# The start of a two-block decoder: memory loaded by whole rows, the identity made on GpSimd, fewer unread products

## The reference, cut to what matters

```python
def rms_norm(x, g):
    xf = x.astype(jnp.float32)
    y = xf * lax.rsqrt(jnp.mean(xf * xf, axis=-1, keepdims=True) + EPS)
    return (y * g.astype(jnp.float32)).astype(x.dtype)
...
def memory_cross_attention(h, m, w_q, w_kv, q_qk_g, k_qk_g, w_o):
    ...
    kv = m @ w_kv
    k = rms_norm(kv[..., :D_MODEL].reshape(B, M, CROSS_HEADS, CROSS_HEAD_DIM), k_qk_g)
    v = kv[..., D_MODEL:].reshape(B, M, CROSS_HEADS, CROSS_HEAD_DIM)
    ...
def first_block(x, mem, positions, ...):
    h = rms_norm(x, attn_norm_g[l])
    proj = h @ w_in[l]
    ...
    x = x + jnp.concatenate([a_out, r_out], axis=-1) @ w_out[l]
    hc = rms_norm(x, cross_norm_g[l])
    m = rms_norm(mem, mem_norm_g[l])
    x = x + memory_cross_attention(hc, m, ...)
    hm = rms_norm(x, moe_norm_g[l])
    x = x + hierarchical_moe(hm, ...)
    return x
```

## Time and profile before

| | us |
|---|---|
| median of 3 runs (939.34 to 940.17) | 940.09 |
| the execution in the profile | 939.83 |
| its span | 937.9 |
| TensorE busy in the span | 928.7 |
| VectorE busy | 743.3 |
| ScalarE busy | 625.3 |
| GpSimd busy | 20.6 |

### The profile page before, as it was taken

One profiled execution on the slowest core, in us unless ns is written; L12 is line 12 of the kernel. 1 busy time (PEld: TensorE's weight loads), 2 busy tenths in 40 slices (PEclk: granted clock), 3 DMA queues, 4 the chain that ended last, 5 costly groups with the idle time before them and its releaser, 6 DMA issues.

```text
span 937.9 us, 13604 instructions
## 1 busy us (share of the span) xinstructions
PE 928.7 (99%) x5027; PEld 804.2 (86%) x5027; DVE 743.3 (79%) x1111; ACT 625.3 (67%) x953; POOL 20.6 (2%) x41
## 2 busy tenths in 40 slices
PE   9999999999999999999999999999999999999997
PEld 7888888888888888888888899999998888888886
DVE  6668686678899999999999889898887655555576
ACT  6785686676878788788778765847574544434456
POOL 2500000000000000000000000000000000000000
PEclk9999999999999999999999999999999999999999
DMA  9865427513799999999998364837457566555531
GB/s 337 245 184 186 146 90 246 186 62 135 247 356 392 352 363 378 354 358 376 341 383 310 103 206 143 258 114 234 154 184 245 178 195 201 185 182 179 184 130 45
DMA packets 102766, 214.50 MB, mean 229 GB/s; under 512 B 5672, under 2 KB 60480, under 8 KB 97088
## 3 DMA queue, kind: packets, MB, share of 16 engines
q1 hardware_dynamic: 101072, 211.70, 64.9%
q0 software_dynamic: 1344, 2.01, 0.8%
q10 hardware_dynamic: 304, 0.20, 0.1%
HBM read 212.84 MB, written 1.05 MB: 228 GB/s over the span
## 4 chain that ended last, share of the span: by engine, by line
PE 92%; DVE 3%; DMA 2%; ACT 1%; SPq 0%; issue 0%; DVEq 0%; ACTq 0%
PE bank L2362 20%; PE bank L2360 20%; PE bank L2361 20%; PE bank L3184 6%; PE bank L3183 6%; PE bank L3182 6%; PE bank L2377 4%; DMA stage<-in_cross_w_kv_dram 2%; PE bank L2373 2%; PE bank L2367 2%; PE bank L2368 1%; PE bank L2714 1%; PE bank L3208 0%; PE bank L3209 0%; PE bank L3210 0%; DVE w_lo L467 0%
## 5 line engine op out<-in xcount | busy, mean ns | idle before, releaser
L2360 PE MATMUL bank<-w_hi,xT_hi 128*128 128x512 f32 (+2 forms) x594 | 234.5, 395 | 0.0
L2362 PE MATMUL bank<-w_hi,xT_lo 128*128 128x512 f32 (+2 forms) x594 | 230.0, 387 | 0.0
L2361 PE MATMUL bank<-w_lo,xT_hi 128*128 128x512 f32 (+2 forms) x594 | 229.7, 387 | 0.0
L465 DVE TENSOR_TENSOR w_lo<-stage,w_hi 128x1024 fp32r<-128x1024 f32 (+3 forms) x94 | 107.5, 1143 | 30.4 <-ACT w_hi L451 29.0
L2362 PEld LDWEIGHTS bank<-w_hi,xT_lo 128*128 128x128 f32 x594 | 111.6, 188 | 22.8
L2360 PEld LDWEIGHTS bank<-w_hi,xT_hi 128*128 128x128 f32 x594 | 112.1, 189 | 20.7 <-DVE w_lo L467 0.2
L2361 PEld LDWEIGHTS bank<-w_lo,xT_hi 128*128 128x128 f32 x594 | 111.8, 188 | 20.8
L3182 PE MATMUL bank<-xT_hi,w_hi 128*128 128x256 f32 x440 | 124.6, 283 | 0.0
L3183 PE MATMUL bank<-xT_lo,w_hi 128*128 128x256 f32 x440 | 124.5, 283 | 0.0
L3184 PE MATMUL bank<-xT_hi,w_lo 128*128 128x256 f32 x440 | 124.5, 283 | 0.0
L451 ACT ACTIVATE w_hi<-stage 128x1024 fp32r<-128x1024 f32 (+3 forms) x96 | 95.5, 995 | 31.4 <-PE bank L2362 13.3
(11 more groups left out here) (492 smaller groups left out, 1579.4 us busy)
## 6 DMA issues: line engine op xcount, KB each, us to landing
stage<-in_w_in_dram SPq DMA_DIRECT2D x36, 1024.0 KB, 5.2
stage<-in_w_gate_up_dram SPq DMA_DIRECT2D x44, 512.0 KB, 4.7
stage<-in_expert_w_gate_dram SPq DMA_DIRECT2D x33, 512.0 KB, 5.4
stage<-in_expert_w_up_dram SPq DMA_DIRECT2D x33, 512.0 KB, 6.5
second<-in_expert_w_down_dram SPq DMA_DIRECT2D x16, 1024.0 KB, 6.5
stage<-in_expert_w_down_dram SPq DMA_DIRECT2D x15, 1024.0 KB, 6.9
stage<-in_w_down_dram SPq DMA_DIRECT2D x11, 1024.0 KB, 4.8
stage<-in_w_out_dram SPq DMA_DIRECT2D x8, 1024.0 KB, 5.1
```

The source lines that it names most:

```text
L465: nc.vector.tensor_tensor(w_lo[:, s, 0:half], src[:, 0:half], w_hi[:, s, 0:half].bitcast(F32), ALU.subtract)
L2360: mm(o, k_hi, v_hi, start=start, stop=False)
L2361: mm(o, k_hi, v_lo, start=False, stop=False)
L2362: return mm(o, k_lo, v_hi, start=False, stop=stop)
```

## The change

- The identity is no longer loaded. GpSimd makes it in place: AFFINE_SELECT takes ones from `one_col` where row equals column and 0 elsewhere, behind a wait for `one_col`.
- The memory comes in two whole row tiles (4 KB per row) in the place of two column halves, both at the head of SyncE's queue. `mem_loaded0` and `mem_loaded1` are now the two row tiles.
- The first quarter of the first weights goes from SyncE's queue to ScalarE's, behind the gain.
- TensorE's first unread products are 6 in the place of 8. It waits for the identity (`ones_set` 2) and for the gain, turns the gain, then turns column blocks 0 to 3 of row tile 0 and, after its landing, of row tile 1. The 2 unread products behind these turns are gone, and the turns of blocks 4 to 7 wait for no load.
- The other waits on `ones_set` count one more.

```diff
--- before.py
+++ after.py
@@ -570,8 +570,6 @@
     def row(v):
         return v.rearrange("(o n) -> o n", o=1)
 
-    first_loads = [(ident, a["const"][:, 0:P]),
-                   (mem_gain_in, a["mem_norm_g"][0].rearrange("(k p) -> k p", p=P))]
     small_loads = [(const[:, P:], a["const"][:, P:])]
     for n, g in enumerate(("attn_norm_g", "cross_norm_g", "moe_norm_g", "g_mix_2", "g_ffn_2", "g_ple_2")):
         small_loads.append((gain_in[KD * n:KD * n + KD], a[g][0].rearrange("(k p) -> k p", p=P)))
@@ -866,22 +864,22 @@
     def store(eng, t, at):
         eng.dma_start(out[0].rearrange("(t p) d -> p t d", p=P)[:, t, at], embed[:, t, at]).then_inc(sem("stored"), 16)
 
+    def first_blocks(eng, k, n):
+        return eng.dma_start(stage[:, 0, 512 * k:512 * (k + n)].rearrange("p (k n) -> p k n", k=n), before[0][0][:, k:k + n])
+
     block = ctx.enter_context(nc.Block())
 
 
     @block.sync
     def _(sp):
-        def memory(c):
-            at = slice(512 * c, 512 * c + 512)
-            sp.dma_start(xs[:, :, at], a["mem"][0].rearrange("(t p) d -> p t d", p=P)[:, :, at]).then_inc(sem(f"mem_loaded{c}"), 16)
+        def memory(t):
+            sp.dma_start(xs[:, t], a["mem"][0][P * t:P * t + P]).then_inc(sem(f"mem_loaded{t}"), 16)
 
         def first_unit(k, n, landed):
-            sp.dma_start(stage[:, 0, 512 * k:512 * (k + n)].rearrange("p (k n) -> p k n", k=n), before[0][0][:, k:k + n])\
-                .then_inc(landed, 16)
-
-        memory(0)
-        first_unit(0, 1, main.landed[0])
-        memory(1)
+            first_blocks(sp, k, n).then_inc(landed, 16)
+
+        for t in range(T):
+            memory(t)
         first_unit(1, 1, main.up_landed[1])
         first_unit(2, 2, main.up_landed[0])
         load_unit(sp, *before[1], 1)
@@ -956,6 +954,9 @@
     @block.gpsimd
     def _(pool):
         nc.gpsimd.memset(one_col[:], 1.0).then_inc(sem("ones_set"), 1)
+        pool.wait_ge(sem("ones_set"), 1)
+        nc.gpsimd.affine_select(out=ident, in_=one_col[:].to_broadcast([P, P]), pattern=[[-1, P]], compare_op=ALU.is_equal,
+                                fill=0.0, base=0, channel_multiplier=1).then_inc(sem("ones_set"), 1)
         pool.wait_ge(sem("x_loaded"), 16)
         for dst, src in small_loads:
             pool.dma_start(dst, src).then_inc(sem("constants_loaded"), 16)
@@ -977,8 +978,8 @@
 
     @block.scalar
     def _(act):
-        for dst, src in first_loads:
-            act.dma_start(dst, src).then_inc(sem("first_loaded"), 16)
+        act.dma_start(mem_gain_in, a["mem_norm_g"][0].rearrange("(k p) -> k p", p=P)).then_inc(sem("mem_gain_loaded"), 16)
+        first_blocks(act, 0, 1).then_inc(main.landed[0], 16)
 
         chain = [0]
 
@@ -1385,7 +1386,7 @@
                 for k in range(KD):
                     act.wait_ge(sem("expert_xg_lo"), bank_parts(k))
                     nc.scalar.activation(later[:, k, 0:T * P], part(k), ACT.Copy, scale=gather_g[:, k:k + 1]).then_inc(sem("later_kept"), 1)
-                act.wait_ge(sem("ones_set"), 3)
+                act.wait_ge(sem("ones_set"), 4)
             first_of = {}
 
             def gates_of(n, at):
@@ -2433,7 +2434,7 @@
             for k in range(4):
                 kk, n, at = 4 * u + k, 2 * u + k // 2, quarter(u, k)
                 if (u, k) == (0, 1):
-                    turn("mem", xs, [("mem_loaded1", 16)], (2, 3))
+                    turn("mem", xs, [], (2, 3))
                 quarter_hi_ready(pe, u, k)
                 high_ready(pe, "mem", n)
                 for t, o in enumerate(outs):
@@ -2522,12 +2523,22 @@
             fills(nc.tensor.transpose(b[:, 0:rows], gain_in, ident[0:rows, 0:rows]), "gains")
 
         pe.wait_ge(sem("unread_set"), 1)
-        unread(8)
-        pe.wait_ge(sem("first_loaded"), 16 * len(first_loads))
+        unread(6)
+        pe.wait_ge(sem("ones_set"), 2)
+        pe.wait_ge(sem("mem_gain_loaded"), 16)
         b = to_fill(pe, "mem_gain")
         fills(nc.tensor.transpose(b[:, 0:KD], mem_gain_in, ident[0:KD, 0:KD]), "mem_gain")
-        turn("mem", xs, [("mem_loaded0", 16)], (0, 1))
-        unread(2)
+        for n in range(2):
+            to_fill(pe, f"mem{n}")
+        view = xs[:].rearrange("p t (k q) -> p t k q", k=KD)
+        for t in range(T):
+            pe.wait_ge(sem(f"mem_loaded{t}"), 16)
+            for n in range(2):
+                b = bank[where[f"mem{n}"][0]]
+                for j in range(2):
+                    ins = transpose(b[:, 256 * j + P * t:256 * j + P * t + P], view[:, t, 2 * n + j])
+                if t == T - 1:
+                    fills(ins, f"mem{n}")
         for c in range(4):
             if c == 0:
                 for u in range(2):
@@ -2625,7 +2636,7 @@
             mm(o, qT_n[:, h, q], kT_n[:, h, keys], start=True, stop=False)
             return mm(o, qT_r[:, h, q], kT_r[:, h // 2, keys], start=False, stop=True)
 
-        pe.wait_ge(sem("ones_set"), 2)
+        pe.wait_ge(sem("ones_set"), 3)
         b = to_fill(pe, "s0")
         for h in range(HEADS):
             ins = score(b[:, P * h:P * h + P], h, slice(0, P), slice(0, P))
```

## The result

| | before | after |
|---|---|---|
| median of 22 runs each, us | 939.84 | 941.60 |
| lowest to highest, us | 939.34 to 941.24 | 940.44 to 943.28 |
| profiled execution: time, span, us | 939.83, 937.9 | 942.47, 940.4 |

The ratio is 1.002, with a 95% interval of 1.0014 to 1.0026: the change costs 1.8 us, where I had forecast 5. It lies inside the range (940.8 to 949.0). The interval lies wholly above 1, so it is slower, but by so little that it still lies inside what I had called the same (938.2 to 942.0).

What follows compares the result with a forecast made beforehand. TensorE, busy 99%, bounds the kernel, so the start of its real products and their clock count. 3.7 + 0.4 + 0 + 1.2 - 0.2 = +5.1 us on 939.8 gave 944.9, stated as 945.0, range 940.8 to 949.0.

Steps and rivals of the forecast that it cites:

- Identity on GpSimd: At the start: a code load before AFFINE_SELECT makes the identity ready at about 9.2, TensorE restarting 3.7 us later.
- the sign against this term: For the identity: AFFINE_SELECT starting within 2 us of the start; for the clock: first real products following at 0.23.
- Memory by whole rows: Start loads: second tile lands between 6.9 and 7.96, before the identity at 9.2, so costs nothing by itself.
- Order of the turns: Memory's first transposes: bank 5 fills after the sixth, not the fourth, so first eviction and product come 0.4 us later.
- Unread products: TensorE's start: taking away two behind the turns gains nothing, and two fewer ahead change nothing.
- Clock: First real products, 12.0 to 14.5: low clock after TensorE's standstill, 0.43 for 0.23 per product, costing 1.2 us.
- a stand of 4.6 us: TensorE idle from 4.54, after its six unread products, until the identity is ready at about 9.2.
- Given back: TensorE's wait for ScalarE at 49.07: a later TensorE finds ScalarE done, winning back 0.2 us.
- the main term: The start's wait for GpSimd's identity, priced with an 8.0 us code load: TensorE restarts 3.7 us later.
- Rival A: Start: code load nothing or short, memory's second tile sets the start; +1.4 start, 1.6 clock, less 0.2: 942.6; chance 0.24.
- Rival B: As the memory-last case, but memory lands by 6.9 to 7.5 and clock is high: 940.4 to 941.0; chance 0.16.
- Slower 0.77: Chance of a measurably slower whole kernel: 0.43 forecast case, 0.14 dearer code load, 0.20 from the memory-last case.

Runs made afterwards that it cites:

- x3_ident: Kernel before with only the identity made by GpSimd's select instead of loaded: 939.65 us, ratio 0.9998.
- x11_rows: Kernel before with memory by whole rows and the weights' first quarter on SyncE's queue behind both tiles, all else as before: 940.53 us, ratio 1.0009.
- x10_fill2: Changed kernel with the 2 unread products put back behind the memory's first turns (6 ahead, 2 behind): 940.23 us, ratio 1.0006.
- x13_ahead8: Changed kernel with 8 unread products ahead of the memory's first turns instead of 6, none behind: 940.26 us, ratio 1.0008.
- x1_fill4: Changed kernel with 4 unread products added behind the memory's first turns: 940.54 us, ratio 1.0008.
- x2_q0sp: Changed kernel with the weights' first quarter back on SyncE's queue, right behind the two memory tiles: 941.54 us, ratio 1.0018.
- x4_q0sp_fill4: Changed kernel with the weights' first quarter on SyncE's queue behind the tiles and 4 unread products behind the turns: 940.55 us, ratio 1.0005.
- x12_hole: Kernel before with GpSimd's identity and, behind the 2 unread products, a TensorE wait for the weights' second quarter: 940.49 us, ratio 1.0009.
- x8_again: Changed kernel, unchanged, run once more for a second profile: 942.68 us, one execution.
- x7_pieces: Kernel before with GpSimd's identity and each column half of the memory issued as two loads of 256 KB: 939.84 us, ratio 0.9999.
- x6_halves_nofill: Kernel before with GpSimd's identity, 6 unread products ahead and none behind the turns, memory still by column halves: 940.03 us, ratio 1.0003.
- x14_hole_nofill: Kernel before with GpSimd's identity, 6 unread products ahead, none behind, and a TensorE wait for the weights' second quarter: 942.90 us, ratio 1.0034.
- x5_mid_fill4: Changed kernel with 4 unread products behind the turns and the weights' first quarter on SyncE's queue between the two memory tiles: 942.26 us, ratio 1.0029.
- x15_ahead8_fill2: Changed kernel with 8 unread products ahead of the memory's first turns and 2 behind: 940.50 us, ratio 1.0007.

## Why the prediction was right or wrong

- **Identity on GpSimd, +3.7: wrong, and the main fault.** The step that failed is "I take it as a load of the code that AFFINE_SELECT needs ... I take 8.0". The row was two instructions of 11 ns; the select started at 0.99, within the 2 us that I had named as the sign against this term, and x3_ident puts the edit at -0.1, no difference that can be told. I had written that the bound from below is nothing, and then chose by a likeness (a DMA's landing) and not by a row of this thing. What I took for 0.2, the select, was 0.29.
- **Memory by whole rows, 0 under cover: wrong without the cover.** The tiles landed at 4.1 and 5.9, below my lower bound of 6.9. I had kept my eye on the memory, and called the quarter of the weights a matter of issue time. It was the quarter, now beside both tiles, that ended last. x11_rows puts whole rows with the quarter behind them at +0.8, two waits on DVE behind the first product among it.
- **Order of the turns, +0.4: not on the path.** The turns ended before the quarter was there.
- **Unread products, 0: wrong.** They "filled the wait for ScalarE" and also kept the clock: with whole rows they are worth 1.0 to 1.4 (after against x10_fill2, x13_ahead8, x1_fill4; x2_q0sp against x4_q0sp_fill4).
- **Clock, +1.2: near in size, but partly by luck.** That products would run at the low level was right: 1.7 in the profiled execution, from 9.9 to 13.3, and by the estimate above about 0.9 in the median one. The reason that I gave did not hold. I had tied it to a stand of 4.6 us that did not come; TensorE stood 1.55 us, and x12_hole shows that a stand of 1.5 does not by itself bring it. In the first profile the first products even ran at the upper level, which I had named as the sign against this term; in x8_again they ran at the lower one.
- **Given back, -0.2: right**, -0.15 at the gains' turn. The turn stood at 51.6 in the kernel after, not near 54, since the main term was missing.
- **Rival A** (no code load, 942.6) was the nearest in mechanism, 1.0 above the result: its +1.4 for the start was +0.5, its 1.6 for the clock 1.7, and the waits on DVE, 0.5, it had not. It watched the landing of the second tile, and the one that counted was the quarter's. Had I given the row its lower bound, this would have been the forecast.
- **Rival B** (940.7) lies 0.9 below the result, by number as near as A. It counted on a clock high from the first products on; in the first profile that held for two pairs only. With two products more ahead the profile of x13_ahead8 shows it high throughout, and the time is 940.26.
- **Slower 0.77** rested on the term that was wrong. By the line that I had drawn at 942.0, 941.6 is the same, to which I had given 0.20.

What stays open: why the quarter's last part lands so late (in the kernel after 6.34 us for 256 KB, while the engines move 215 to 223 GB/s from 5 to 7 us; in x7_pieces 8.06), why DVE gets it anywhere from 7.14 (x10_fill2) to 7.89 with the same loads, and what sets the moment at which the clock changes, since two profiles of one kernel differ in it. Two things are mixed there: a rise that comes late (x8_again, x4_q0sp_fill4, x6_halves_nofill, x10_fill2) and a fall after a rise (the kernel after, x2_q0sp, x14_hole_nofill). Whether in x14_hole_nofill the products themselves or the 0.6 us of longer standing decides was not told apart there; x13_ahead8 alone speaks for the products.

## What to carry to other kernels

An instruction that the trace of before does not show gets its price from its own lower bound until a run shows more; put it alone into the kernel before, and the largest term of the sum is settled in one run. A first load must be judged by the bytes that have to be in before the first real product: 768 KB by column halves here, 1280 by whole rows, and the piece that comes last counts, with all that its engine does behind it. Products that nobody reads may be what keeps the clock up while loads land: take them away and the price appears elsewhere, later, and not in every execution.

## What was unexpected of the hardware

- Whole rows land faster than column halves. In the ten profiles with whole rows the first tile of 512 KB landed 3.3 to 3.8 us after its issue, in the six with column halves the first half of 512 KB took 4.2 to 4.8 (4.6 in the earlier trace rows). In x5_mid_fill4 the quarter is issued second, as with column halves, and the tile still took 3.5. The change had this gain and could not use it, for the quarter.
- The select of 128x128 on GpSimd took 0.29 us, its setup twice 11 ns, and was ready at 1.3; the load of the identity that it replaces cost nothing that can be told either (x3_ident, -0.1).
- The clock. In the kernel after and in x2_q0sp TensorE did only turns between about 4.7 and 8, and ran 3.3 to 3.4 us of the first real work at 1.2 GHz in one profile of each, 5.7 us in x8_again. With two to four products beside the turns it was at 2.4 GHz from the first real product on in four of the six profiles with whole rows and the tiles issued first (x1_fill4, x11_rows, x13_ahead8, x15_ahead8_fill2), and low until about 10.0 in x4_q0sp_fill4 and 10.7 in x10_fill2. The turns themselves run at either level: eight in 1.03 us in x1_fill4, in 1.91 in x8_again.
